# RWKV-7 recurrence in chunks of 64 tokens, directions in sequence, two tiles' inverses by common instructions

## Chip, cores, metric

The kernel runs on one core of a Trainium2 chip. The metric is the device time of the program in microseconds, the median of several runs. A profiled execution of the same program gives the trace.

## What is computed

One inference step of a layer: RMS norm and modulation, one input projection, a bidirectional RWKV-7 mixing group of 8 heads of 64 channels and a bidirectional S5 group beside it, an output projection and an MLP, over 1024 latent and 128 context tokens. The part that matters here is the RWKV-7 scan, for each head and direction:

```python
def step(S, inp):
    r_t, w_t, k_t, v_t, ma_t, b_t = inp          # ma = -kk, b = kk * a
    sa = jnp.einsum('dbhij,dbhj->dbhi', S, ma_t)
    S = S * w_t[..., None, :] + sa[..., None] * b_t[..., None, :] + v_t[..., None] * k_t[..., None, :]
    return S, jnp.einsum('dbhij,dbhj->dbhi', S, r_t)
s_last, ys = lax.scan(step, jnp.moveaxis(s0.astype(f32), 1, 0), xs)   # direction 1 on flipped tokens
y = ys[0] + flip(ys[1])
```

The context's tokens are scanned first from a zero state, and their last state is an output; the latent tokens start from a cached state. All of this stage is computed in float32.

## The kernel before

The program is a sequence of stages. Each stage is a block in which every engine runs its own queue in order, with semaphores between them; behind the block GpSimd clears the stage's semaphores, one instruction each (`clear`, L328). `stage_rwkv` (L1651) runs a loop of four passes over groups of 128 channels (two heads): `stage_prepare`, `stage_chunks`, `stage_finish`.

`stage_prepare` (L993) makes, for each direction, four operands of 128 channels by 1152 tokens, `R.x[d]`, laid out as 9 tiles of 128 tokens with 4 operands each (a, r, b, k, already scaled by the decays), the values `R.v`, and per tile the factors `R.pre`, `R.post` and `R.step` by which the state is carried on.

`stage_chunks` (L1181) works through the tiles of 128 tokens. Both directions go side by side: a step takes the next tile of each. A tile has two parts of work. The inverse: `turn` (L1295) transposes b and k and makes b·a for the two halves of 64 tokens; `score` (L1308) makes the 128x512 products of all tokens with all, for both heads; VectorE masks them (L1487); `start_inverse`, and five levels of `merge_q` (L1325) and `merge_x` (L1335), build the inverse of a unit triangular matrix of 64 tokens, for both heads and both halves, by blocks of 2, 4, ... 64. Each level goes TensorE (`merge_q`), ScalarE (L1469, eviction), TensorE (`merge_x`), VectorE (L1554, addition). The small products are 64x64, on diagonal quarters of the array (`blocks`, L1289). The recurrence: `right_side` (L1346), `solve_first` (L1358) for the first half, `carry` to the second, `solve_second`, `advance` (the state after the tile) and `output` (L1391). In a step the recurrence of the former tile is interleaved with the inverse of the next one, at fixed places between the levels. So there are ten steps: one with inverses alone, eight with both, one with the recurrence alone. Steps 3 to 8 are run by a loop of three rounds with two steps each, whose tiles are addressed by registers; GpSimd copies each tile's operands to a fixed place first (L1265 to L1274), and clears y at the head of the stage (L1255), to which both directions add their output (L1528). GpSimd also makes the masked blocks of all levels in one product (L1279).

`stage_finish` (L1564) normalises `y`, adds the bonus, multiplies by the gate and transposes.

In the trace a float32 multiplication is two MATMUL records.

Of the kernel before, what the change touches and what calls it, by code (L numbers as in the profile page):

```python
# [14 lines left out]
P = 128  # L15
# [977 lines left out]
def stage_prepare(nc, M, ins, ct):  # L993
# [10 lines left out]
    m, tot, step = A.take(NB), A.take(NB), A.take(NB)  # L1004
# [3 lines left out]
    tiles = lambda v: v.rearrange("p (b t) -> p b t", b=NB)  # L1008
    three = lambda v: v.rearrange("p (g c) -> p g c", g=TG)
    with ExitStack() as ctx:  # L1010
# [109 lines left out]
        def _(dve):  # L1120
# [19 lines left out]
            for d in range(2):  # L1140
                x = R.x[d]
# [17 lines left out]
                op(stt(out=x[:, :, 2, :], in0=tiles(kn), scalar=-1.0, in1=tiles(a), op0=ALU.mult, op1=ALU.mult))  # L1159
                op(ts(x[:, :, 3, :], tiles(a), par[:, 1:2], omka, ALU.mult, ALU.add))  # L1160
                op(tt(x[:, :, 3, :], x[:, :, 3, :], tiles(k), ALU.mult))
                for n, (src, v) in enumerate(((kn, e), (r, t))):
                    dve.wait_ge(ev("exp"), 3 * d + n + 1)
                    tt(x[:, :, n, :], tiles(src), tiles(v), ALU.mult).then_inc(ev("x"), 1)
                dve.wait_ge(ev("exp"), 3 * d + 3)
                for n in (2, 3):
                    tt(x[:, :, n, :], x[:, :, n, :], tiles(e), ALU.mult).then_inc(ev("x"), 1)

                dve.wait_ge(ev("edge"), 2 * d + 2)
                op(nc.vector.tensor_copy(step, R.post[d]))  # L1170
                if d == 0:
                    op(tt(step[:, 0:LB - 1], R.post[d][:, 0:LB - 1], R.pre[d][:, 1:LB], ALU.mult))
                else:
                    op(tt(step[:, 1:LB], R.post[d][:, 1:LB], R.pre[d][:, 0:LB - 1], ALU.mult))
                op(tt(R.step[d], step.unsqueeze(2).broadcast_to([P, NB, 2]),
                      M.head_ind.unsqueeze(1).broadcast_to([P, NB, 2]), ALU.mult))
# [4 lines left out]
def stage_chunks(nc, M, ins, outs, ct):  # L1181

# [3 lines left out]
    D2, H2 = range(2), range(2)  # L1193
    double = lambda *shape: [[A.take(*shape) for _ in D2] for _ in range(2)]
    st = double(4, P)
    vs = double(P)
    tm = double(3, P)
    xx = double(2, 2, 64)
    ar = double(2, 2, P)
    mt = [[[A.take(2, 2, P) for _ in range(2)] for _ in D2] for _ in range(2)]  # L1200
    lo = [A.take(2, NLEV - 1, 64) for _ in D2]
    qs = [A.take(2, 64) for _ in D2]
    rs = [A.take(2, 64) for _ in D2]
    u = [A.take(2, 64) for _ in D2]
    p = [A.take(2, 64) for _ in D2]
    pt = [A.take(2, 64) for _ in D2]
    enter = [A.take(2) for _ in D2]
    h0 = A.take(2, 64)
    fin = A.take(2, 64)
    half = [slice(0, 64), slice(64, P)]  # L1210
    flat = lambda v: v.rearrange("p h c -> p (h c)")

    SPREAD, BESIDE = ((1, 0), (1, 1), (0, 0), (0, 1)), (1, 2)
    INV = lambda d: ps[:, 2 + d]
    REC = lambda d: ps[:, 4 + d]
    PROD = lambda d, j: ps[:, 6 * d + j]
    with ExitStack() as ctx:
# [3 lines left out]
        def steps(eng, body, new=False, old=False):  # L1223


            def known(s):
                latent = lambda t: (t, LB - 1 - t) if t >= 0 else (LB, LB)
                body(lambda o: s + o, s % 2, latent(s - 1) if s <= LB else None, latent(s - 2) if s else None)
            for s in range(3):
                known(s)  # L1230
            with eng.Fori(1, LB // 2) as i:
                count = [eng.snap(i * 2 + o) for o in range(4)]
                for s in (1, 2):
                    tiles = [None, None]
                    for n, wanted in enumerate((new, old)):
# [4 lines left out]
        def first(eng):  # L1240

            eng.wait_ge(ev("y_clear"), 1)
# [1003 lines left out]
```

## Time and profile before

| | us |
|---|---|
| median of 3 runs | 3204.84 (3203.38 to 3208.48) |
| the profiled execution | 3206.6 |
| its span, first to last instruction | 3204.8 |
| TensorE busy | 2222.1 (69%), 19956 records |
| VectorE busy | 1513.0 (47%) |
| ScalarE busy | 690.0 (22%) |
| GpSimd busy | 652.4 (20%) |
| mean granted TensorE clock | 0.832 |

The busy times are of the whole span; a stage can be bound by another engine than the program. Engines are named PE (TensorE), PEld (its weight loads), DVE (VectorE), ACT (ScalarE), POOL (GpSimd), SP (SyncE). A "q" behind a name is the engine's sequencer. Times in a timeline are microseconds from the span's start. The granted clock 1.00 is 2.4 GHz, 0.50 is 1.2 GHz.

### The profile page before, as it was taken

The numbers are of one execution on the slowest core, as the hardware profiler recorded it, in microseconds if no ns is written. First come the engines' busy times: TensorE is split into PE (matmuls) and PEld (weight loads), VectorE is DVE, ScalarE is ACT, GpSimd is POOL, SyncE is SP. The second block draws the span as 40 slices with busy tenths as digits, with TensorE's granted clock in tenths as the row PEclk, the third lists the DMA queues.
The fourth block names the chain that finished last, engine by engine and source line by source line (L and its number), as shares of the span: only waits on it lengthen the run. The fifth ranks groups of instructions, "written<-read, shape, count | busy, mean of one in ns | idle before, by whom it ended". The sixth has DMA issues, their size and how long they took to land. (4 is left out here: it accounts for less than half of the span.)

```text
span 3204.8 us, 49900 instructions
## 1 busy us (share of the span) xinstructions
PE 2222.1 (69%) x19956; PEld 1392.6 (43%) x19956; DVE 1513.0 (47%) x2768; ACT 690.0 (22%) x1436; POOL 652.4 (20%) x585
## 2 busy tenths in 40 slices
PE   7406411332374994579665995499479999999998
PEld 1104211232242773357543773277335555555553
DVE  0360679776306553555526552655334333332335
ACT  0211100111212331233213321233123321211221
POOL 0200613300211221022111211122042211110134
PEclk9657556665686997789877996699689999999999
DMA  7410000000000000000000000000233111100112
GB/s 266 168 35 26 7 1 7 7 7 18 20 23 1 3 1 18 7 3 1 2 23 2 2 0 25 1 3 0 94 118 132 53 53 53 53 18 36 53 47 99
DMA packets 61998, 119.09 MB, mean 37 GB/s; under 512 B 4359, under 2 KB 24327, under 8 KB 61451
## 3 DMA queue, kind: packets, MB, share of 16 engines
q1 hardware_dynamic: 61852, 116.92, 10.7%
q8 instruction: 120, 1.97, 0.3%
q14 instruction: 26, 0.21, 0.0%
HBM read 104.53 MB, written 10.27 MB: 36 GB/s over the span
## 5 line engine op out<-in xcount | busy, mean ns | idle before, releaser
L82 PE MATMUL psum<-arena 128*128 128x384 bf16 (+2 forms) x2244 | 742.1, 337 | 293.9 <-POOL arena L375 79.4
L83 PE MATMUL psum<-arena 128*128 128x384 bf16 (+2 forms) x2244 | 743.2, 338 | 0.0
L84 PE MATMUL psum<-arena 128*128 128x384 bf16 (+2 forms) x2244 | 743.1, 338 | 0.0
L82 PEld LDWEIGHTS psum<-arena 128*128 128x128 bf16 (+1 forms) x2244 | 227.1, 101 | 472.0 <-issue 80.4
L1292 PE MATMUL psum<-arena 64*64 64x64 f32 x8640 | 359.1, 222 | 27.6 <-ACT arena L1469 8.5
L1292 PEld LDWEIGHTS psum<-arena 64*64 64x64 f32 x8640 | 303.7, 134 | 68.6 <-issue 46.3
L84 PEld LDWEIGHTS psum<-arena 128*128 128x128 bf16 (+1 forms) x2244 | 226.9, 101 | 174.7 <-issue 16.1
L83 PEld LDWEIGHTS psum<-arena 128*128 128x128 bf16 (+1 forms) x2244 | 225.2, 100 | 172.3 <-issue 13.1
L2026 DVE TENSOR_TENSOR arena<-arena 128x384 f32<-128x384 f32 x96 | 103.2, 1075 | 236.5 <-ACT arena L1893 236.5
L724 PE MATMUL psum<-arena 128*16 128x128 f32 (+1 forms) x128 | 29.7, 319 | 265.4 <-ACT arena L667 265.4
L1469 ACT ACTIVATE arena<-psum 128x128 f32<-128x128 f32 x360 | 95.7, 278 | 415.1 <-PE psum L1292 411.0
L1554 DVE TENSOR_TENSOR arena<-arena,psum 128x256 f32<-128x256 f32 (+1 forms) x360 | 139.6, 395 | 64.2 <-PE psum L1292 58.0
L2041 DVE TENSOR_TENSOR arena<-arena,psum 128x512 f32<-128x512 f32 x108 | 74.5, 690 | 195.9 <-PE psum L84 195.9
L1313 PE MATMUL psum<-arena 128*128 128x512 f32 x288 | 157.0, 654 | 5.3 <-ACT arena L1441 5.3
L1302 PE MATMUL psum<-arena 128*128 128x128 f32 x144 | 32.5, 310 | 161.3 <-ACT arena L1449 153.2
L724 PEld LDWEIGHTS psum<-arena 128*16 128x16 f32 (+1 forms) x128 | 18.9, 177 | 268.3 <-issue 266.9
L1279 POOL TENSOR_TENSOR arena<-arena 128x640 f32<-128x640 f32 x72 | 97.6, 1374 | 138.5 <-ACT arena L1453 138.5
L1947 POOL TENSOR_TENSOR arena<-arena 128x1024 bf16<-128x1024 f32 x32 | 63.8, 2027 | 260.7 <-ACT arena L1873 260.7
L1953 POOL TENSOR_TENSOR arena<-arena 128x4096 bf16<-128x4096 f32 x8 | 59.5, 7437 | 279.9 <-ACT arena L1885 279.9
L636 POOL TENSOR_TENSOR arena<-arena 128x960 f32 (+1 forms) x32 | 70.9, 2247 | 165.7 <-PE psum L697 165.6
L1272 POOL COPY arena<-arena 128x128 f32 (+1 forms) x72 | 23.2, 322 | 388.6 <-PE psum L1398 388.6
L1487 DVE TENSOR_TENSOR arena<-psum,arena 128x512 f32<-128x512 f32 x144 | 95.2, 680 | 9.4 <-PE psum L1313 9.4
(295 smaller groups left out, 3386.0 us busy)
## 6 DMA issues: line engine op xcount, KB each, us to landing
arena<-in_w_ff SPq DMA_DIRECT2D x16, 2048.0 KB, 8.7
arena<-in_w_ada SPq DMA_DIRECT2D x12, 2048.0 KB, 8.0
arena<-in_x SPq DMA_DIRECT2D x18, 512.0 KB, 3.7
arena<-in_pos SPq DMA_DIRECT2D x18, 512.0 KB, 4.7
arena<-in_w_in SPq DMA_DIRECT2D x12, 512.0 KB, 4.1
x<-arena SPq DMA_DIRECT2D x9, 512.0 KB, 3.1
arena<-x SPq DMA_DIRECT2D x9, 512.0 KB, 3.3
out_y<-arena SPq DMA_DIRECT2D x9, 512.0 KB, 2.6
```

Of the source, the lines that this page charges most:

```text
L82: nc.tensor.matmul(out, whi, xhi, start=first, stop=False)
L83: nc.tensor.matmul(out, wlo, xhi, start=False, stop=False)
L84: return nc.tensor.matmul(out, whi, xlo, start=False, stop=last)
L636: mult = lambda o, x, y: nc.gpsimd.tensor_tensor(o, x, y, ALU.mult)
L1279: nc.gpsimd.tensor_tensor(lo[d], tm[q][d][:, 2].rearrange("p (h c) -> p h c", h=2).unsqueeze(2) .broadcast_to([P, 2, NLEV - 1, 64]), M.lev ...
L1292: last = mm(out[half[b]], lhs[half[b]], rhs[half[b]], start=True, stop=True)
L1313: mm(PROD(d, j), st[q][d][:, 2 + j], ar[q][d].rearrange("p h m t -> p (h m t)"), start=True, stop=True)\
L1469: nc.scalar.activation(flat(qs[d]), INV(d)[:, 0:P], ACT.Copy).then_inc(ev("q_read", d, l), 1)
L1487: tt(mt[q][d][j].rearrange("p h m t -> p (h m) t"), PROD(d, j).rearrange("p (m t) -> p m t", m=4), M.score_mask[:, d], ALU.mult).then_inc( ...
L1554: tt(xd, xd, z[:, :, ms], ALU.add).then_inc(ev("x", d, l), 1)
L2026: nc.vector.tensor_tensor(f[N % 3], f[N % 3], f[N % 3], ALU.mult).then_inc(ev("square"), 1)
L2041: nc.vector.tensor_tensor(a, a, ps[:, 6 + h, :], ALU.add).then_inc(ev("acc"), 1)
```

## The change

The order becomes a sequence of 18 units, a unit being one tile in one direction: the nine of direction 0 (context first), then the nine of direction 1. Units are taken in pairs, nine pairs in each pass, and the code of all is written out, with constant addresses. Both units' inverses are made by the same evictions and additions. The recurrence goes in chunks of 64 tokens, two for each unit, 36 in a row, each of `enter`, `solve` and `leave`. A body `i` holds the inverses of pair `i` and the four chunks of pair `i - 1`.

- Preparation stores `R.x[d]` as 8 slots of 64 tokens per tile, so that a and r of one half, and b and k of one half, are neighbours; `R.step` has one factor per tile.
- `score` makes, for each head and half, 128x128 products within the half (64 rows of the array, 128 columns). Six buffers `mt` hold the masked scores.
- The levels: `merge_q` for both units, then VectorE's `copy_predicated` puts the masked part into `grow` (an identity elsewhere, from GpSimd at the head), `merge_x` for both units, then ScalarE copies the whole bank to `xx`. GpSimd's product of all levels' blocks goes; it makes the first blocks `xt0` in eight small operations a pair.
- `turn` transposes b and k by multiplication with the identity, for `leave` alone.
- ScalarE writes each chunk's output to `R.y[d]`; nothing is added there. `stage_finish` adds the two directions at its head.
- The loop, the copies to a fixed place, the clearing of y and the wide masks go. The stage uses 46 semaphores instead of 107.

The core of the diff; what is left out is the old bodies and the counterparts of these functions on the other engines:

```diff
-                x = R.x[d]
+                x = [R.x[d][:, :, at] for at in (slice(1, 3), slice(0, 4, 3), slice(5, 7), slice(4, 8, 3))]
...
-                op(tt(R.step[d], step.unsqueeze(2).broadcast_to([P, NB, 2]),
-                      M.head_ind.unsqueeze(1).broadcast_to([P, NB, 2]), ALU.mult))
...
+def unit(u):
+    d, s = u // NB, u % NB
+    return d, s, LB if s == 0 else (s - 1 if d == 0 else LB - s)
...
+            def merge_q(i, l):
+                pe.wait_ge(ev("x0_read") if l == 1 else ev("x", l - 1), i + 1)
+                for q in H2:
+                    for h in H2:
+                        for f in H2:
+                            r = upper(f)
+                            last = mm(qblock(r, q, h), mt[(2 * i + q) % 6][r, h, f, 1 - f], xx[r, q, h, 0], start=True, stop=True)
+                last.then_inc(ev("q", l), 1)
+            def merge_x(i, l):
+                pe.wait_ge(ev("q_read", l), i + 1)
+                for q in H2:
+                    for h in H2:
+                        for f in H2:
+                            r = upper(f)
+                            xt = xt0[r, q, h] if l == 1 else xx[r, q, h, 1]
+                            if l < NLEV - 1:
+                                mm(xblock(r, q, h, 0), xt, grow[r, l - 1, q, h], start=True, stop=True)
+                            last = mm(xblock(r, q, h, 1), grow[r, l - 1, q, h], xt, start=True, stop=True)
+                last.then_inc(ev("xq", l), 1)
...
+            def enter(g):
+                pe.wait_ge(ev("state"), g + 1)
+                need(pe, ev("y_read"), g)
+                for h in H2:
+                    last = mm(MIX[upper(f), h, mixcol(f)], slot(x, f, 0)[half[h]], state[g % 4][half[h]], start=True, stop=True)
+                last.then_inc(ev("enter"), 1)
+            def solve(g):
+                pe.wait_ge(ev("w"), g + 1)
+                pe.wait_ge(ev("x_last"), g // 4 + 1)
+                for h in H2:
+                    last = mm(MIX[r, 0, 128 + 64 * h:192 + 64 * h], xf[par][r, q, h], w[g % 2][r, h], start=True, stop=True)
+                last.then_inc(ev("u"), 1)
+            def leave(g):
+                pe.wait_ge(ev("u_read"), g + 1)
+                pe.wait_ge(ev("uv"), 2 * (g // 2) + 2)
+                pe.wait_ge(ev("tm"), g // 4 + 1)
+                for h in H2:
+                    last = mm(PUT[half[h]], tm[par][q][:, f, half[h]], uv[par][q][:, f, half[h]], start=True, stop=True)
+                last.then_inc(ev("put"), 1)
+                for h in H2:
+                    mm(MIX[half[f], h, mixcol(f)], slot(x, f, 1)[half[h]], state[g % 4][half[h]], start=True, stop=False)
+                    last = mm(MIX[half[f], h, mixcol(f)], mt[g // 2 % 6][:, h, f, f], uv[par][q][:, f, half[h]],
+                              start=False, stop=True)
+                last.then_inc(ev("y"), 1)
...
+            def body(i):
+                inv, old, front = i < PAIRS, i > 0, i + 1 < PAIRS
+                g = 4 * (i - 1)
...
```

With both parts present, TensorE's order in a body is: leave(g-1), begin, enter(g), local, merge_q 1, solve(g), merge_x 1, leave(g), merge_q 2, enter(g+1), merge_x 2, solve(g+1), turn, merge_q 3, leave(g+1), merge_x 3, enter(g+2), score, merge_q 4, solve(g+2), merge_x 4, leave(g+2), score, merge_q 5, enter(g+3), merge_x 5, solve(g+3). The eviction of merge_q on VectorE (where both units have one direction), the first blocks on GpSimd, and the head of `stage_finish`:

```diff
+            def merged(i, l):
+                reset(i, l)
+                dve.wait_ge(ev("q", l), i + 1)
+                nc.vector.copy_predicated(grow[:, l - 1].rearrange("p q h c -> p (q h) c"),
+                                          where[:, 1 - d0, l:l + 1].broadcast_to([P, 4, 64]),
+                                          Q[:, 0:4 * 64].rearrange("p (b c) -> p b c", b=4)).then_inc(ev("q_read", l), 1)
...
+            def first_block(u):
+                pool.wait_ge(ev("masked"), u + 1)
+                need(pool, ev("xq", 1), u // 2)
+                for f in H2:
+                    r = upper(f)
+                    masked.step(tt(xt0[r, q], mt[u % 6][r, :, f, 1 - f], M.level_mask[r, d, 0:1].broadcast_to([64, 2, 64]),
+                                   ALU.mult))
+                    masked.settle(pool)
+                for f in H2:
+                    r = upper(f)
+                    first.step(tt(xt0[r, q], xt0[r, q], M.ident64[r].unsqueeze(1).broadcast_to([64, 2, 64]), ALU.add))
+                    first.settle(pool)
...
+            op(tt(y, y, R.y[1], ALU.add))
```

`xt0` must be there for `begin`, which is the start of the next pair's inverses; its scores are made in the body before.

## Rows read from the trace of the kernel before

**Rows 1.** Windows: stretch: us, busy us and records of each engine, PEclk, DMA share, GB/s.
```profile
1028.00:1240.00 212.00, 189.73 (x2916) 143.33 (x2916) 116.58 (x280) 64.69 (x216) 47.40 (x93) 0.97 0.01 2
1031.00:1035.00 4.00, 2.53 (x12) 1.17 (x12) 1.82 (x3) 2.33 (x8) 2.38 (x5) 0.50 0.01 2
1040.00:1050.00 10.00, 8.92 (x215) 7.53 (x216) 3.99 (x10) 2.69 (x10) 0.00 (x0) 1.00 0.01 2
1073.46:1095.10 21.64, 20.71 (x326) 15.78 (x326) 12.50 (x30) 7.21 (x25) 5.08 (x10) 1.00 0.01 3
1570.00:1577.00 7.00, 5.38 (x48) 4.64 (x46) 3.08 (x12) 0.00 (x0) 0.00 (x0) 1.00 0.00 0
1915.00:1922.00 7.00, 6.90 (x38) 6.64 (x37) 2.22 (x8) 0.00 (x0) 0.00 (x0) 0.52 0.00 0
315.00:335.00 20.00, 19.28 (x63) 11.21 (x63) 0.00 (x0) 5.90 (x11) 0.00 (x0) 0.50 0.00 1
```
**Rows 2.** Timeline of TensorE: start, duration; heads of two successive full steps.
```profile
1094.92 0.41 PE L1302 MATMUL psum<-arena 128*128 128x128 f32 x2 [0.20 <-DVE arena L1554]
...
1116.39 0.30 PE L1302 MATMUL psum<-arena 128*128 128x128 f32 x1 [0.21 <-DVE arena L1554]
```
**Rows 3.** Timeline: first and last operation of the first and third pass.
```profile
1028.10 1.06 POOL L1255 MEMSET arena<- 128x1152 f32 x1 [76.85 <-POOLq L330]
...
1232.18 0.28 DVE L1528 TENSOR_TENSOR arena<-arena,psum 128x128 f32<-128x128 f32 x1
...
1714.70 1.06 POOL L1255 MEMSET arena<- 128x1152 f32 x1 [76.85 <-POOLq L330]
...
1923.27 0.28 DVE L1528 TENSOR_TENSOR arena<-arena,psum 128x128 f32<-128x128 f32 x1
```
**Rows 4.** Timeline of TensorE: heads of the last step, same passes.
```profile
1224.16 0.46 PE L1353 MATMUL psum<-arena 128*128 128x128 f32 x2 [0.24 <-DVE arena L1554]
...
1912.25 0.46 PE L1353 MATMUL psum<-arena 128*128 128x128 f32 x2 [0.24 <-DVE arena L1554]
```
**Rows 5.** Timeline: one level of both directions' merges in the first step.
```profile
1043.72 0.28 ACT L1469 ACTIVATE arena<-psum 128x128 f32<-128x128 f32 x1 [1.68 <-PE psum L1292]
...
1045.92 0.28 ACT L1469 ACTIVATE arena<-psum 128x128 f32<-128x128 f32 x1 [1.45 <-PE psum L1292]
```
**Rows 6.** Timeline in a full step: 16 records on 64x64 quarters, twice.
```profile
1114.58 0.68 PE L1292 MATMUL psum<-arena 64*64 64x64 f32 x16
...
1115.50 0.68 PE L1292 MATMUL psum<-arena 64*64 64x64 f32 x16 [0.24 <-ACT arena L1469]
```
**Rows 7.** Groups by line and form: count, busy us, mean ns, idle before.
```profile
L1554 DVE TENSOR_TENSOR arena<-arena,psum 128x256 f32<-128x256 f32 x72 | 30.0, 422 | 11.1 <-PE psum L1292 9.7
L1469 ACT ACTIVATE arena<-psum 128x128 f32<-128x128 f32 x90 | 23.9, 278 | 103.8 <-PE psum L1292 102.8
L1487 DVE TENSOR_TENSOR arena<-psum,arena 128x512 f32<-128x512 f32 x34 | 22.4, 679 | 0.3 <-PE psum L1313 0.3
L1279 POOL TENSOR_TENSOR arena<-arena 128x640 f32<-128x640 f32 x16 | 21.6, 1370 | 32.4 <-ACT arena L1453 32.4
L1453 ACT ACTIVATE arena<-psum 128x384 f32<-128x384 f32 x16 | 7.9, 492 | 5.0 <-PE psum L1304 5.0
L1554 DVE TENSOR_TENSOR arena<-arena,psum 128x128 f32<-128x128 f32 x18 | 4.8, 289 | 4.9 <-PE psum L1292 4.8
L1272 POOL COPY arena<-arena 128x128 f32 x12 | 3.8, 317 | 83.4 <-PE psum L1398 83.4
L1606 ACT ACTIVATE arena<-psum 128x512 f32<-128x512 f32 x2 | 1.2, 599 | 17.1 <-PE psum L84 17.1
```
**Rows 8.** Timeline of TensorE: changes of form, in the S5 stage and in a full step.
```profile
315.72 0.45 PE L401 MATMUL psum<-arena 128*128 128x128 f32 x1 [10.71 <-ACT arena L365]
...
316.10 0.28 PE L402 MATMUL psum<-arena 16*128 16x16 f32 x1
...
1112.24 1.15 PE L1292 MATMUL psum<-arena 64*64 64x64 f32 x32
...
1113.32 0.49 PE L1395 MATMUL psum<-arena 128*128 128x128 f32 x2
```
**Rows 9.** Timeline: VectorE's products from SBUF, before and beside GpSimd's.
```profile
1117.73 0.29 DVE L1535 TENSOR_TENSOR arena<-arena 128x128 f32<-128x128 f32 x1 [1.23 <-ACT arena L1453]
...
1118.06 1.29 DVE L1538 TENSOR_TENSOR arena<-arena 128x128 f32<-128x128 f32 x1
```
**Rows 10.** Timeline at the stages' borders; one full-width addition of the final stage.
```profile
1025.18 0.18 DVE L1175 TENSOR_TENSOR arena<-arena 128x18 f32<-128x18 f32 x1
...
1028.27 2.11 DVE L1478 MEMSET arena<- 128x512 f32 x4 [2.91 <-PEq L330]
...
1240.94 1.35 DVE L1628 TENSOR_REDUCE arena<-arena 128x18 f32<-128x1152 f32 x1 [8.48 <-PEq L330]
...
1251.87 1.35 DVE L1636 TENSOR_TENSOR arena<-arena 128x1152 f32<-128x1152 f32 x1
```

More of the change, by code:

```diff
@@ L1003, in stage_prepare @@
     r, k, kn, a, lw, c_, e, t = (A.take(T) for _ in range(8))
-    m, tot, step = A.take(NB), A.take(NB), A.take(NB)
+    m, tot = A.take(NB), A.take(NB)
     hb = A.take(4)
@@ L1221, in stage_chunks @@
         block = ctx.enter_context(nc.Block())
[L1223 to L1235, printed above, removed]
-                        tiles[n] = (eng.snap(i * 2 + (s - 1 - n)), eng.snap(LB - s + n - i * 2)) if wanted else (i, i)
-                    body(lambda o, s=s: count[s + o], s % 2, *tiles)
-            known(LB + 1)
-        def first(eng):
-            eng.wait_ge(ev("y_clear"), 1)
         @block.sync
@@ L1433, in _, with score @@
-            pe.wait_ge(ev("p_clear"), 2)
-            steps(pe, body)
+            def score(u):
+                d, s, tile = unit(u)
+                q, x = u % 2, R.x[d][:, tile]
+                need(pe, ev("masked"), u)
+                if q == 0:
+                    need(pe, ev("lkv"), u)
+                for f in H2:
+                    for h in H2:
+                        at = 2 * P * q + P * f
+                        last = mm(SCORE[:, h, at:at + P], kb(x, f)[half[h]], ar(x, f)[half[h]], start=True, stop=True)
+                last.then_inc(ev("score"), 1)
@@ L1470, in _, with begun, local @@
-            act.wait_ge(ev("ar_clear"), 4)
-            steps(act, body)
+            copy = lambda out, src: nc.scalar.activation(out, src, ACT.Copy)
+            def begun(i):
+                act.wait_ge(ev("x0"), i + 1)
+                copy(xx[:, :, :, 0], X.rearrange("p (q h n c) -> p q h n c", q=2, h=2, n=2)[:, :, :, 0]).then_inc(ev("x0_read"), 1)
+            def local(i):
+                act.wait_ge(ev("local"), i + 1)
+                for f in H2:
+                    r = upper(f)
+                    src = ps[r, f, :].rearrange("p (q c) -> p q c", q=2)[:, :, 0:P]
+                    copy(wv[i % 2][r], src).then_inc(ev("lkv"), 1)
@@ L1560, in stage_chunks @@
+            nc.vector.memset(state[0], 0.0).then_inc(ev("state"), 1)
+            mask(0)
+            mask(1)
+            dve.wait_ge(ev("grow"), 1)
+            for i in range(PAIRS + 1):
+                body(i)
+            advanced(4 * PAIRS - 1)
     clear(nc, ev)
```

600 lines of the change are left out of this document (309 added, 291 removed).

## The prediction

> **What bounds the kernel now.** The page's slices and the windows by stage come first. The four passes of the recurrence stage (one for each group of two heads) are a quarter of the program: TensorE is busy 189.7 of 212 us in a pass, at a granted clock of 0.97 [rows 1]. The timeline of TensorE then shows what a step costs: a full step, from one turn of the operands to the next, takes 21.47 us [rows 2], and TensorE is busy 20.71 of 21.64 us in one [rows 1]. So before the change these stages are bound by TensorE's queue; VectorE (12.5 us a step), ScalarE (7.2) and GpSimd (5.1) have room [rows 1]. A pass runs from GpSimd's first MEMSET to VectorE's last addition: 204.4 us in the first and 208.9 in the third [rows 3]; the second and the fourth, read in the same way, lie between, and the mean of the four is 206.3. There are 8 full steps, a first one before them (inverses alone) and a last one (recurrence alone), 8.3 us [rows 4].
>
> The third pass is longer because its last step took 11.3 us against 8.3 [rows 4]: TensorE's granted clock there was 0.52, the 1.2 GHz level, against 1.00, the 2.4 GHz level, in the same step of the second pass [rows 1]. So in one pass the clock held through 7 us in which the engine was busy for 5.38, and in the other it fell in the same work. In the full steps and in the first step's merges (8.92 of 10 us busy) the clock stayed at 1.00 [rows 1].
>
> **The sizes of a hop.** In the first step the merges stand alone, and one level for both directions is 2.20 us (ACT at 1043.72, then at 1045.92) [rows 5]. The parts add up to that: 8 records on 64x64 quarters, half of such 16, take 0.45 us to their end (16 take 0.68, two quarters side by side [rows 6], and 32 take 1.15 [rows 8]), 0.04 to ScalarE's start, 0.28 for its copy [rows 7], 0.15 back to TensorE, 0.64 for 16 that wait for nothing else, 0.04 to VectorE, 0.42 for the addition of 256 columns [rows 7], 0.15 back: 2.17. So I trust such sums for the new chain. Evictions by columns: ScalarE 0.28 for 128, 0.49 for 384, 0.60 for 512, hence 0.385 for 256; VectorE 0.29 for 128, 0.42 for 256, 0.68 for 512, hence 0.22 for 64 [rows 7].
>
> **What one change of form costs on TensorE.** Where a matrix multiplication has another number of active rows or columns than the one before, it starts 0.07 us before the former's end and never earlier: 316.10 against an end at 316.17, and 1113.32 against 1113.39 [rows 8]; without a change the next pair of records follows 0.058 after the start of the former (32 records in 1.15). I found this at every change of form at which work was waiting, some 600 of them, all with 128x128 or 16x128 on one side. The new recurrence alternates 64x64 with 128x64, which no row shows directly. The Trainium skill, "TensorEngine Tiling (Array Packing)", Key Properties, says that a change of tiling mode drains TensorE; by that rule every alternation pays, and the trace agrees for the forms that it shows.
>
> **The new body, for two tiles of one direction.** TensorE's records do not get fewer: 180 multiplications or 360 records a body, against 326 for two tiles before [rows 1]. What falls is the 128x512 scores and the count of evictions; what is added is a recurrence of 4 successive steps a body, in place of two directions side by side.
> One level of both inverses at once: merge_q 16 records, 0.67; 0.04; copy_predicated of 256 columns, 0.42; 0.15; merge_x 32 records, 1.14; 0.04; ScalarE's copy of 512 columns, 0.60; 0.15: 3.21 us. copy_predicated is in no row: I take the addition of 256 columns, as it reads as many PSUM columns; the ends are the 128-column addition, 0.29, and the 512-column product, 0.68.
> One `leave` is put, then state part and score part for each head in turn: 128x64, 64x64, 128x64, 64x64, 128x64. Each piece is two records (0.107 to the second) and then the change (0.218 less 0.07): 0.255, five times, 1.28 us. Four leaves are 5.1 us of TensorE a body.
> Beside a level's ScalarE or VectorE hop TensorE has 0.8 to 0.9 us free. In the order of the code: begin to the first merge 1.24; level 1 3.21 and 0.42 because leave(g) doesn't fit; level 2 3.21 and 0.40 for the turn (8 records at 0.112 and two changes); level 3 3.21 and 0.60 for leave(g+1); level 4 3.21 and 1.00 for leave(g+2) and a score; level 5 to the end of the next leave 4.10 (merge_q, the predicated copy behind a mask, merge_x of 16, ScalarE 0.385 and 0.28 one after the other, leave 1.28). Sum 20.6 us against 21.47. TensorE is occupied 17 to 18 of it, so the four leaves decide.
> A pass: 7.0 us to the first begin (h0's DMA, the grow copy, and eight GpSimd operations of 0.40 with 0.10 between, where 640 columns take 1.37 and a copy of 128 0.32 [rows 7]); first body 16.9 (1.24, four levels, 2.8); 8 bodies of 20.6 and 1.5 in all for the resets and the split copies where the direction changes, 166.3; last, recurrence alone: 4 steps of 1.8 (leave, until ScalarE has freed the MIX columns), 0.79 (enter to solve) and 0.91 (solve to put), 13.8 with its end. Sum 204.0 at the full clock, 2.3 less than the mean before.
>
> **Clock.** The first body starts at 1.2 GHz, as before (0.50 in that stretch [rows 1]), but has no 128x512 scores ahead, and its merges wait more: at that level throughout it would cost 7.3 us more, at the other nothing; I take 4. In the full bodies TensorE is occupied some 0.87 of the time, as in the last steps of before, of which two of four fell, at 3.0 us a fall [rows 4]. If none falls, 0; if all run at 1.2 GHz, 30.2 us a body, so 77 a pass. I take about one fall a pass, 3.5; and 1.5 for the last body. Together 9.0 a pass.
>
> **GpSimd beside VectorE.** A VectorE product from two SBUF operands took 1.29 us beside GpSimd's 128x640 product [rows 9], against 0.29 for the one just before it. The predicated copy has its mask in SBUF and its data in PSUM, like the additions with a PSUM operand, which keep 0.42. The Trainium skill, "SBUF — State Buffer", says that GpSimd and a VectorE operation with two SBUF inputs exclude each other on one pair of ports; by it this copy goes free, and the trace agrees for the additions. I add 1.0 a pass for what the copy may be above 0.42 or held up (ends -4, +9, from the two rows).
>
> **Outside the pass.** After a pass GpSimd clears the stage's semaphores: VectorE is idle 8.48 us behind it, and 2.91 after the preparation [rows 10]. I count 107 semaphores and 28, so 0.07 us each; the new stage has 46, hence 4.0: 4.4 less. The final stage gains one addition of 1152 columns at its head, 1.35 and 0.04 [rows 10]: 1.4 more. Preparation writes the same columns in runs of 64 and loses two operations of 0.18 [rows 10]: 0.4 less; nothing hides any of these three. The clearing of y goes, 1.06 [rows 3], but h0's DMA is then late. Half of the score masks' constants go from the first DMA: nothing. Unrolling: steps in straight-line code took 21.6, in the loop 21.5 to 21.8 over its jump: nothing, ±0.3 a body.
>
> **Sum.** A pass: -2.3 + 9.0 + 1.0 - 4.4 + 1.4 - 0.4 = +4.3 us, four times +17. The profiled execution is 3206.6 us (span 3204.8), so 3223.8; the median of the runs is 1.8 below it: 3222.
>
> **Rivals.**
> (1) 64x64 and 128x64 follow each other without the drain. Leave is then some 0.7 us, a body 18.5 and a pass 185, 18.9 less: 3222 - 76 = 3146, faster. For: no row with that pair. Against: every other pair drains. It decides where a leave is under 0.9 us. 0.10.
> (2) As forecast, but the clock stays up or recovers within the first body: 9.0 a pass less, 3186, faster. For: the first body of before. 0.15.
> (3) The clock falls in a third or more of the full bodies: +25 a pass or more, 3322 and up (3500 if in all). For: the rows 315.72 on, where two forms alternate and TensorE is busy 19.28 of 20 us at a clock of 0.50 [rows 1, 8]. 0.17.
> (4) The predicated copy takes 0.68 or is held by GpSimd: +9 a pass, 3258. 0.08.
> (5) "Common instructions" don't overlap in TensorE's quarters (enter's and score's two row halves one after the other): 0.7 us a body, +24, 3246; kept in the forecast's own range, 3190 to 3265. Forecast 0.50, of which 0.08 below 3198 and 0.12 within 0.2%, which is about what a measurement of this kernel can tell from no change.
> Faster 0.33, same 0.12, slower 0.55. The range, 3150 to 3330, leaves out the lower part of (1) and the upper of (3).
>
> **What would show it.** In the new profile: begin to begin 20.6 us; the five pieces of a leave at 0.255; copy_predicated at 0.42; gap behind the pass 4.0; clock row of the passes. If leave is 0.7, rival 1; if the clock of a pass is under 0.85, rival 3; if the gap between merge_q's end and merge_x is above 0.7, rival 4. A body that is long by waits that I haven't named (GpSimd's first_block late for begin, which I put 1.6 us ahead of its need) would make the working wrong even at the right time.

## The result, and the profile after

| | us |
|---|---|
| median after | 3212.85 (3208.91 to 3219.81, 8 runs) |
| median before, same chip | 3204.19 (3200.61 to 3208.48, 8 runs) |
| ratio after/before | 1.0027, 95% [1.0016, 1.0037] |
| the profiled execution after | 3210.29, span 3208.5 |
| forecast | 3222 (3223.8 in the profile) |

The change makes the kernel slower, by 8.7 us (0.3%) in the medians and by 3.7 us between the two profiled executions; the forecast had 18 and 17. The sign and most terms stand, but the sum is more than twice too large. The windows of the four passes, from GpSimd's first operation to ScalarE's last, come first (columns as in [rows 1]).

```profile
1028.34:1242.25 213.91, 182.96 (x3240) 153.97 (x3240) 51.29 (x153) 59.59 (x162) 49.79 (x129) 0.89 0.01 3
1377.00:1587.17 210.17, 178.94 (x3240) 150.11 (x3240) 51.17 (x153) 59.59 (x162) 49.78 (x129) 0.91 0.01 3
1722.05:1932.47 210.42, 179.11 (x3240) 150.24 (x3240) 51.17 (x153) 59.59 (x162) 49.80 (x129) 0.91 0.01 3
2066.78:2277.38 210.60, 179.19 (x3240) 150.31 (x3240) 51.17 (x153) 59.59 (x162) 49.80 (x129) 0.91 0.01 3
```

A pass takes 211.3 us in the mean (206.3 before, 214.0 forecast). TensorE has more records (3240 against 2916 [rows 1]) and less busy time; VectorE's busy time is under half of what it was. The granted clock of a pass is 0.89 to 0.91, where it was 0.97 in the first pass [rows 1]. Where that clock goes is seen in shorter windows of TensorE alone (its busy time, PEclk, DMA share, GB/s): the start of the first body of the second pass, the piece in which it comes back, a full body, the head of the second body of the first pass, and the last body.

```profile
1384.00:1394.00 10.00, 8.15 (x130) 0.50 0.01 2
1394.00:1399.00 5.00, 4.42 (x66) 0.70 0.00 0
1405.00:1425.39 20.39, 18.47 (x360) 1.00 0.01 2
1058.00:1062.00 4.00, 3.80 (x78) 0.63 0.01 4
1572.00:1587.00 15.00, 11.26 (x68) 0.50 0.00 1
```

The full bodies run at 2.4 GHz nearly throughout. In this pass the inverses' first 13 us are at 1.2 GHz: the mean of 0.70 between 1394 and 1399 puts the clock's return at 1397, and the first begin is at 1383.76. The last body is at 1.2 GHz in all four passes, but for its first 1 us. In the first pass the clock fell twice within full bodies (windows with all engines, columns as in [rows 1]):

```profile
1059.10:1062.40 3.30, 3.15 (x50) 2.97 (x51) 0.44 (x1) 1.02 (x3) 0.00 (x0) 0.50 0.02 5
1062.60:1079.50 16.90, 15.38 (x277) 12.78 (x272) 4.80 (x14) 4.83 (x13) 5.33 (x14) 1.00 0.01 2
1079.60:1082.90 3.30, 3.17 (x58) 2.99 (x60) 0.74 (x2) 1.61 (x5) 0.00 (x0) 0.50 0.00 0
```

Each fall lasted 3.4 us, and the two bodies took 21.57 and 21.33 in place of 20.39: 1.2 and 0.9 us more. The timeline of the second pass gives the lengths: GpSimd's first operation, the heads of the first four bodies and of the eighth full one (`begin`, L1259), ScalarE's last.

```profile
1377.00 1.25 POOL L1484 COPY arena<-arena 128x1280 f32<-128x1280 f32 x1 [76.48 <-POOLq L330]
...
1383.76 0.80 PE L1259 MATMUL psum<-arena 64*64 64x64 f32 x10 [3.50 <-POOL arena L1501]
...
1405.01 0.51 PE L1259 MATMUL psum<-arena 64*64 64x64 f32 x10 [1.01 <-POOL arena L1501]
...
1425.40 0.27 PE L1259 MATMUL psum<-arena 64*64 64x64 f32 x2
...
1445.79 0.32 PE L1259 MATMUL psum<-arena 64*64 64x64 f32 x3
...
1549.52 0.68 PE L1259 MATMUL psum<-arena 64*64 64x64 f32 x16
...
1586.89 0.27 ACT L1405 ACTIVATE arena<-psum 64x128 f32<-64x128 f32 x1 [2.19 <-PE psum L1338]
```

The first begin comes 6.8 us after the start (forecast 7.0), the first body takes 21.25 (22.72 in the first pass), a full body 20.39 (forecast 20.6; the two with the direction's change and its resets take 21.2, two behind them 20.48), and from the eighth full body's head to the end it is 37.64. The row at 1405.01 has one thing more in its brackets: the second begin waited 1.01 us for GpSimd, a wait that the forecast had named only as a sign of being wrong.

One leave, in the second full body (to hold against [rows 8]):

```profile
1428.91 0.34 PE L1334 MATMUL psum<-arena 128*64 128x64 f32 x4
1429.18 0.33 PE L1337 MATMUL psum<-arena 64*64 64x64 f32 x2
1429.43 0.33 PE L1338 MATMUL psum<-arena 128*64 128x64 f32 x2
1429.69 0.32 PE L1337 MATMUL psum<-arena 64*64 64x64 f32 x2
1429.95 0.33 PE L1338 MATMUL psum<-arena 128*64 128x64 f32 x2
1430.20 0.68 PE L1280 MATMUL psum<-arena 64*64 64x64 f32 x16
```

Each piece starts 0.25 to 0.27 us after the former, 1.29 in all: the forecast's 5 x 0.255. (The forecast took each piece as two records. The put has four, and takes 0.27 all the same.) The groups by form in the first pass, and the borders of the final stage behind the second:

```profile
L1572 DVE COPY_PREDICATED arena<-arena,psum 128x256 f32<-128x256 int32 x40 | 17.7, 442 | 53.8 <-PE psum L1280 53.7
L1577 DVE COPY_PREDICATED arena<-arena,psum 128x128 f32<-128x128 int32 x10 | 2.5, 296 | 4.9 <-PE psum L1280 4.9
...
1591.06 1.36 DVE L1714 TENSOR_TENSOR arena<-arena 128x1152 f32<-128x1152 f32 x1 [5.61 <-PEq L330]
...
1596.64 1.35 DVE L1719 TENSOR_REDUCE arena<-arena 128x18 f32<-128x1152 f32 x1 [1.23 <-ACT arena L1695]
```

The predicated copy takes 0.44 (forecast 0.42), never more. From the end of the pass (1586.89 + 0.27) to 1591.06 it is 3.90 us (3.88 to 4.10 in the four), where it was 8.23 to 8.48; forecast 4.0.

### The profile page after: what moved, and what is told of

It is laid out like the page before. It is cut to its first block and busy times, and to the rows that moved or that the text cites. A ratio compares the mean times of both kernels' runs of the same rounds, so it can differ in the third digit from the quotient of the medians.

```text
span 3208.5 us, 50188 instructions
## 1 busy us (share of the span) xinstructions
PE 2174.9 (68%) x21252; PEld 1417.5 (44%) x21252; DVE 1253.9 (39%) x2256; ACT 669.6 (21%) x1220; POOL 663.4 (21%) x729
## 5 line engine op out<-in xcount | busy, mean ns | idle before, releaser
L1405 ACT ACTIVATE arena<-psum 64x128 f32<-64x128 f32 (+3 forms) x648 | 238.4, 380 | 628.7 <-PE psum L1293 302.0
L1292 PE MATMUL psum<-arena 64*64 64x64 f32 x2304 | 162.8, 233 | 44.0 <-DVE arena L1572 37.8
L1293 PE MATMUL psum<-arena 64*64 64x64 f32 x2880 | 180.1, 224 | 17.9 <-DVE arena L1572 14.9
L1293 PEld LDWEIGHTS psum<-arena 64*64 64x64 f32 x2880 | 158.1, 140 | 22.8 <-DVE arena L1572 19.3
L1292 PEld LDWEIGHTS psum<-arena 64*64 64x64 f32 x2304 | 137.4, 138 | 62.2 <-DVE arena L1572 52.4
L1572 DVE COPY_PREDICATED arena<-arena,psum 128x256 f32<-128x256 int32 x160 | 70.6, 441 | 212.0 <-PE psum L1280 211.5
L1248 PE MATMUL psum<-arena 64*128 64x128 f32 x576 | 56.1, 317 | 142.4 <-PEq L330 139.2
L1496 POOL TENSOR_TENSOR arena<-arena 64x128 f32<-64x128 f32 x144 | 64.8, 450 | 329.2 <-issue 258.3
L1280 PE MATMUL psum<-arena 64*64 64x64 f32 x2880 | 129.0, 232 | 5.6 <-ACT arena L1405 5.0
L1280 PEld LDWEIGHTS psum<-arena 64*64 64x64 f32 x2880 | 103.6, 141 | 24.7 <-ACT arena L1405 12.3
```

What stands on the lines that cost most here:

```text
L1280: last = mm(qblock(r, q, h), mt[(2 * i + q) % 6][r, h, f, 1 - f], xx[r, q, h, 0], start=True, stop=True)
L1292: mm(xblock(r, q, h, 0), xt, grow[r, l - 1, q, h], start=True, stop=True)
L1293: last = mm(xblock(r, q, h, 1), grow[r, l - 1, q, h], xt, start=True, stop=True)
L1405: copy = lambda out, src: nc.scalar.activation(out, src, ACT.Copy)
L1496: masked.step(tt(xt0[r, q], mt[u % 6][r, :, f, 1 - f], M.level_mask[r, d, 0:1].broadcast_to([64, 2, 64]), ALU.mult))
L1572: nc.vector.copy_predicated(grow[:, l - 1].rearrange("p q h c -> p (q h) c"), where[:, 1 - d0, l:l + 1].broadcast_to([P, 4, 64]), Q[:, 0:4 ...
```

## Experiments

Times are medians, ratios are against the kernel before on the same chip. Unless said otherwise the base is the kernel after.

### The changes of form: two runs

```diff
                 for h in H2:
-                    mm(MIX[half[f], h, mixcol(f)], slot(x, f, 1)[half[h]], state[g % 4][half[h]], start=True, stop=False)
-                    last = mm(MIX[half[f], h, mixcol(f)], mt[g // 2 % 6][:, h, f, f], uv[par][q][:, f, half[h]],
-                              start=False, stop=True)
+                    mm(MIX[half[f], h, mixcol(f)], mt[g // 2 % 6][:, h, f, f], uv[par][q][:, f, half[h]],
+                       start=True, stop=False)
+                for h in H2:
+                    last = mm(MIX[half[f], h, mixcol(f)], slot(x, f, 1)[half[h]], state[g % 4][half[h]], start=False, stop=True)
```

The second run has the same two loops with the state parts first, as in the code of the change (four changes of form).

> The changed kernel, with the order inside a leave turned round: put, then the score parts of both heads, then the state parts of both heads, so that TensorE changes its form twice in a leave in place of six times; same multiplications, same waits. Theory A (each change of form drains TensorE and leaves sit on the path): a leave is 6 records at 0.058 apart and 4 such with two changes, 0.76 us against 1.28; four of them a body give 20.4 - 2.2 = 18.2 to 18.4 us from begin to begin, 19.5 us less a pass, about 3210 - 78 = 3132 us in the profile, 0.976 of the kernel before. Rival B (the changes of form lie beside the evictions' waits and cost the body nothing): body 20.4, 3210 us. In between, if the score now stands in the way of the next merges: body near 19.3, 3172 us.

> The changed kernel with a leave ordered as put, both state parts, both score parts: four changes of form in place of six. Theory A (cost goes by the number of changes): a body of 18.8 to 19.0 us, 14 us less a pass, about 3210 - 57 = 3153 us; two thirds to three quarters of what two changes give. Rival B (not the changes but the waits decide): the same time as the changed kernel, 3210. If a gain comes from the order of the parts alone and not from the number of changes, this one and the one with two changes give the same.

Measured: 3122.3 us (3118.3 to 3123.4), ratio 0.9741 [0.9724, 0.9758]; and 3161.8 us, 0.9868 [0.9852, 0.9885]. A full body takes 17.98 with two changes and 18.83 with four, against 20.39 with six: 2.4 and 1.56 less. A leave of the first, and the heads of two bodies:

```profile
1710.66 0.34 PE L1334 MATMUL psum<-arena 128*64 128x64 f32 x4
1710.83 0.40 PE L1337 MATMUL psum<-arena 128*64 128x64 f32 x4
1711.15 0.33 PE L1340 MATMUL psum<-arena 64*64 64x64 f32 x4
1711.42 0.68 PE L1280 MATMUL psum<-arena 64*64 64x64 f32 x16
...
1725.02 0.27 PE L1259 MATMUL psum<-arena 64*64 64x64 f32 x1
...
1743.00 0.27 PE L1259 MATMUL psum<-arena 64*64 64x64 f32 x1
```

And the same leave in the second run, with four changes:

```profile
1391.65 0.34 PE L1334 MATMUL psum<-arena 128*64 128x64 f32 x4
1391.91 0.33 PE L1337 MATMUL psum<-arena 64*64 64x64 f32 x4
1392.18 0.45 PE L1339 MATMUL psum<-arena 128*64 128x64 f32 x4
1392.55 0.68 PE L1280 MATMUL psum<-arena 64*64 64x64 f32 x16
```

The same six multiplications take 1.29 us with six changes, 0.90 with four and 0.76 with two. The four leaves of a full body, each from its put to the next work, take 5.17, 3.60 and 2.69 together: 1.57 and 2.48 less, which is what the bodies lose, 1.56 and 2.41. Theory A holds for both in this: the drain between 64x64 and 128x64 is real (the forecast's first rival is out), and the leaves lie on the path. The price does not go by the number of changes alone, though. A put is followed after 0.27 us by another form and after 0.17 by its own, so one change costs 0.10. The larger part of what the second run gains is that like parts are neighbours: the state parts of both heads, four records, take 0.27 together, where two records took 0.26. A score part adds to what the state part wrote, which would be another cause of its late start; but the next state part, which adds to nothing, starts as late (0.26 and 0.26 in the rows of the change), so that is not it. The rule of the Trainium skill, "TensorEngine Tiling (Array Packing)", Key Properties, that a change of tiling mode drains the engine, holds here too, between two modes that both use 64 columns; the page gives no price, these rows give 0.10 us for one change alone and 0.53 for the whole leave.

### What the common instructions are worth

```diff
-                    copy(xx.rearrange("p q h n c -> p (q h n c)"), X).then_inc(ev("x", l), 1)
+                    for q in H2:
+                        last = copy(xx[:, q].rearrange("p h n c -> p (h n c)"), X[:, 2 * P * q:2 * P * q + 2 * P])
+                    last.then_inc(ev("x", l), 1)
...
-                if d0 == d1:
+                if False:
```

> The changed kernel, in which ScalarE and VectorE evict the inverses of the two directions' tiles by an instruction for each tile (two of 256 columns in place of one of 512; two predicated copies of 128 in place of one of 256), TensorE's work unchanged. Theory A (the level's chain of evictions sets the body, so common instructions are what gained): ScalarE 2 x 0.38 + 0.05 against 0.597 and VectorE 2 x 0.298 against 0.441 give 0.3 to 0.37 a level; the levels that have no TensorE work to hide it give 0.9 us a body, 7.7 a pass, 3210 + 31 = 3241 us. Rival B (TensorE's own queue sets the body and covers the evictions): 3210 us within 4.

(The first and the last copy of a body are split in the same way.)

Measured: 3231.4 us (3230.4 to 3232.3), 1.0084 [1.0067, 1.0101], 18.5 above the change: half of A's 31. A full body is 20.80, so 0.4 longer and not 0.9. The pairs of instructions show why (ScalarE, then VectorE):

```profile
1454.05 0.66 ACT L1405 ACTIVATE arena<-psum 128x256 f32<-128x256 f32 x2 [1.37 <-PE psum L1293]
...
1452.00 0.50 DVE L1583 COPY_PREDICATED arena<-arena,psum 128x128 f32<-128x128 int32 x2 [1.18 <-PE psum L1280]
```

Two copies of 256 columns take 0.66 together, where one takes 0.38 and one of 512 takes 0.60; two predicated copies of 128 take 0.50, where one takes 0.30 and one of 256 takes 0.44. So an instruction starts before the former's end, and the split costs 0.06 + 0.06 a level, not 0.35. The Trainium skill has figures for both engines: "ScalarE: Activation LUTs", What ACT_TABLE_LOAD costs, has successive ACTIVATEs overlap by about 93 ns; in these rows it is 0.10 us (twice 0.38 less 0.66). "Vector Engine (DVE) Microarchitecture Reference", 5.2, gives VectorE 1.0417 ns a column and about 75 ns an instruction in a queue, so by it a second copy of 128 columns would add 0.21 us, an estimate; in these rows it adds 0.20. Eight bodies a pass make 13 us of the 18.5. For the other 5.5 the trace has falls of the clock: one body took 25.91 us, with a fall of 13.7 us in it, and five others 0.9 more than their like, 9.5 us in all against 2.1 in the trace of the change.

### The clearing of semaphores

```diff
+            for n in range(61):
+                ev("idle", n)
```

> The changed kernel with 61 more semaphores in the recurrence stage's list, which nobody signals and which are cleared with the others behind each pass, 107 in all as in the kernel before. Theory A (the gap behind a pass is GpSimd clearing one semaphore after another, 0.07 us each): gap 8.2 to 8.5 in place of 3.9 to 4.1, 4.4 us a pass, 3210 + 17.5 = 3227.5 us, 1.0055 of the changed kernel. Rival B (the gap of before was the loop's end or the transfers, not the count): gap unchanged, 3210 us.

Measured: 3229.0 us (3225.8 to 3232.8), 1.0079 [1.0061, 1.0098], 16.2 more than the change. The same border as above:

```profile
1599.24 1.36 DVE L1716 TENSOR_TENSOR arena<-arena 128x1152 f32<-128x1152 f32 x1 [9.43 <-PEq L330]
```

The pass ended at 1591.53, so the gap is 7.71 in place of 3.90: 0.062 us for each of 61. Theory A stands, the price a little under the 0.07 taken; the run below with 15 fewer has 2.82, 0.072 for each. But with the 107 semaphores of before the gap is 7.7 us and not 8.2 to 8.5: the count makes 3.8 us of the 4.35 by which the gap shrank, and the other 0.5 stays unexplained.

### The addition in the final stage

```diff
-            op(tt(y, y, R.y[1], ALU.add))
```

> The changed kernel without the addition of the two directions' outputs at the head of the final stage (1152 columns on VectorE; the output of the second direction is left out of the result). Theory A (nothing hides it, as forecast): 1.39 us a pass less, 3210 - 5.6 = 3204.7 us. Rival B (TensorE's gate work and ScalarE's copies in that stage end later than the addition, so part of it was hidden; the stage grew by 0.9 and not 1.4 between the two kernels): 0.9 a pass or less, 3206.5 to 3210 us.

Measured: 3211.7 us (3205.6 to 3221.4, 12 runs), 1.0019 [1.0010, 1.0028]: too near to the change to tell in the total, the more so as the profiled execution (3216.6) had seven short falls of the clock and that of the change two. The rows of the stage tell: from the end of the second pass to GpSimd's first operation of the final stage, a power that waits for VectorE's sums, it is 10.14 us in place of 11.12, 0.98 less. VectorE's second sum of this run:

```profile
1594.85 1.35 DVE L1718 TENSOR_REDUCE arena<-arena 128x18 f32<-128x1152 f32 x1 [1.65 <-ACT arena L1695]
```

It waits 1.65 us for ScalarE's square, against 1.23 with the addition: without the addition ScalarE is still evicting the gates when the square's input is ready, and 0.4 of the addition's 1.39 lay beside that. Rival B, nearly: 0.98 where it had 0.9 or less.

### The clock at the head and at the tail of a pass: two runs

```diff
+            def fill(tiles, bank):
+                for b in H2:
+                    mm(ps[half[b], bank, 0:tiles * P], M.ident64[half[b]], R.v[half[b], 0:tiles].rearrange("p b c -> p (b c)"),
+                       start=True, stop=True)
...
                     merge_x(i, 1)
+                    if i == 0:
+                        fill(2, 5)
```

(the same behind levels 2 to 4, and `fill(4, 5)` twice before the first body; in the second run `fill(2, 4)` behind each `enter` and `solve` of the last body alone)

> The changed kernel, with multiplications that nobody reads put into TensorE's idle time before the first begin (4 of 64x512 in all) and behind each of the first four levels of a pass's first body (2 of 64x256 each), so that the engine waits less there. In the changed kernel the first body ran at a granted clock of 0.50 for its first 10 to 13 us and took 21.24 us (22.7 in the first pass). Theory A (the engine's waits in that body keep the clock down, and a filled one gets it back earlier): first body 17 to 19 us, 2 to 4 us less a pass, 3210 - 8 to 17 = 3193 to 3202 us. Rival B (the clock comes back when it does, whatever the engine did): the fillers cost what they take at the low clock where they stand in a merge's way, 0 to 2 us a pass more, 3210 to 3218 us.

> The changed kernel, with multiplications that nobody reads (2 of 64x256) behind each enter and each solve of a pass's last body, where TensorE waits for VectorE and ScalarE. In the changed kernel that body ran at a granted clock of 0.50 in all four passes and took 37.67 us from its begin of the eighth full body to the end, 3.3 more than worked out at the full clock. Theory A (the waits of the last body make the clock fall): begin of the eighth to the end 34.4 to 35.5, 2 to 3.3 us less a pass, 3210 - 9 to 13 = 3197 to 3201 us. Rival B (it falls for what came before, in the eighth full body, or the fillers don't suffice): the fillers stand in the way of solve and leave at the low clock, 0 to 3 us a pass more, 3210 to 3222 us.

Head: 3197.3 us (3194.7 to 3200.4, 10 runs), 0.9975 [0.9966, 0.9984], so 0.25% faster than the kernel before. The first body takes 18.12 in all four passes:

```profile
1377.90 0.27 PE L1259 MATMUL psum<-arena 64*64 64x64 f32 x2 [0.55 <-POOL arena L1517]
...
1396.01 0.51 PE L1259 MATMUL psum<-arena 64*64 64x64 f32 x10 [1.13 <-POOL arena L1517]
```

Theory A: the granted clock is 1.00 from the first begin on, where it was 0.50 for 13 us. The second begin still waits 1.13 us for GpSimd, so that is no matter of the clock.

Tail: 3213.1 us (3198.5 to 3218.1), 1.0024 [1.0008, 1.0040], no different from the change. Behind it stand two cases. From the eighth head to the end the passes took 39.91, 39.75, 33.56 and 33.55 us, against 37.76 in the mean without fillers; the second and the third (windows in the last body, columns as in [rows 1]):

```profile
1571.00:1586.00 15.00, 13.64 (x86) 8.38 (x84) 1.60 (x6) 1.64 (x6) 0.59 (x2) 0.50 0.00 1
1918.00:1933.00 15.00, 12.63 (x132) 7.63 (x128) 2.28 (x9) 2.84 (x10) 0.59 (x2) 1.00 0.01 1
```

In two passes the clock stayed at 1.00 and 4.2 us were gained, in two it fell all the same and the fillers cost 2.1. Neither theory alone; what tells the two cases apart stays open. (The two in which it stayed up are those whose first body took the long 22.6 to 22.7; no run shows whether the one hangs on the other.)

### Do more waits bring the clock of the full bodies down?

```diff
+    spare = A.take(4 * P)
...
+                    copy(spare, X)
                     copy(xx.rearrange("p q h n c -> p (q h n c)"), X).then_inc(ev("x", l), 1)
```

> The changed kernel in which ScalarE evicts the inverses' X twice in levels 1 to 4 (once to a tile nobody reads), 0.45 to 0.6 us more in each, so that TensorE waits longer in every full body. Theory A (waits of that size don't bring the clock down; the body only grows by them): 21.6 to 22.8 us a full body, +10 to 19 us a pass, 3250 to 3287 us. Rival B (the third rival of the forecast: with more waits the clock falls in a third or more of the full bodies): 25 us and more for those, 3330 us and up.

Measured: 3231.8 us (3230.7 to 3233.6), 1.0081 [1.0062, 1.0099], under what either theory gave. A pair of copies takes 1.08 in place of 0.60:

```profile
1453.08 1.08 ACT L1406 ACTIVATE arena<-psum 128x512 f32<-128x512 f32 x2 [1.34 <-PE psum L1294]
```

Four times 0.49 are put in, and a full body grows by 0.49; by the order of the code, TensorE's leaves, turn and scores stand beside the copies of the other levels. Of the 28 full bodies that can be read from head to head, eight took a further 0.9, each with one fall of 3.4 us in it. So there are two falls a pass with more waits, in this one trace, and one costs about 1 us, not the 10 of a body that is all at 1.2 GHz: the engine is back at 2.4 GHz within the body. That is where rival 3 of the forecast fails, by its price.

### The late first blocks, and a better kernel: four runs

Fifteen semaphores fewer (one count for all levels in place of one each), with the grouped leaves:

```diff
-                pe.wait_ge(ev("q_read", l), i + 1)
+                pe.wait_ge(ev("q_read"), 5 * i + l)
```

and for the others, in the first body only, the same with `mask` on VectorE:

```diff
                     merge_x(i, 1)
+                if i == 0:
+                    score(2)
...
                     merge_x(i, 2)
+                if i == 0:
+                    score(3)
...
-                if front:
+                if front and old:
                     score(2 * i + 2)
```

> The kernel with the parts of a leave grouped (two changes of form in place of six, 3122.3 us median, 3123 in its profile) and, beside it, 15 semaphores fewer in the recurrence stage: those of the five levels are one count each (31 in all in place of 46). Theory A (clearing costs 0.07 us each): the gap behind a pass 2.9 in place of 4.0 us, 4.3 us less in all, 3118 us; 0.9728 of the kernel before. Rival B (15 fewer change nothing, or the counts cost in the body): 3122 us or above.

> The changed kernel with the early scores and masks of tiles 2 and 3 in the first body alone, no fillers, leaves and semaphores as in the change. Theory A (GpSimd's masking of the first blocks is what the second begin waits for, 1.0 us in the trace, at either clock): 1 us less a pass, 3210 - 4 = 3206 us; the wait of the second begin for GpSimd gone. And if the busier start brings the clock back earlier, up to 3 us more a pass, 3194 us. Rival B (another wait comes last there): first body unchanged at 21.2 us, 3210 us.

> The kernel with grouped leaves and 15 semaphores fewer (3113 us median), with two more edits in each pass's first body only: the scores and masks of tiles 2 and 3 come behind levels 1 and 2 in place of 3 and 4, and fillers (multiplications nobody reads) stand before the first begin and behind levels 3 and 4. Theory A: with the clock up, the first body is 18.1 us because the second begin waits 1.1 us for GpSimd, which masks the first blocks of tiles 2 and 3 only after their late scores; with early scores that wait goes and the body is 16.9 to 17.3 us against 21.2 to 22.7, 4 us less a pass: 3113 - 16 = 3097 us, 0.967 of the kernel before. Rival B (the early scores and masks stand in the way of merges, or the clock doesn't come back): 18 to 21 us for the body, 3100 to 3113 us.

> The kernel of the run called early, and the fillers behind each enter and solve of the last body as well. In the changed kernel those fillers kept the clock up in two passes of four (33.6 us from the eighth begin to the end against 37.7) and cost 2.2 us in the two in which it fell. Theory A (with bodies less full of waits ahead of it the clock holds): 3 to 4 us less a pass, 3097 - 14 = 3083 us. Rival B (as often up as down): 1 us less a pass, 3093 us. Rival C (it falls always, for what comes before): 2.2 more a pass, 3106 us.

| run | median | ratio, 95% |
|---|---|---|
| grouped_few | 3112.9 (3108.6 to 3130.0) | 0.9727 [0.9702, 0.9751] |
| early_only | 3205.9 (3200.8 to 3211.3) | 1.0002 [0.9991, 1.0013] |
| early | 3097.5 (3095.0 to 3098.1) | 0.9660 [0.9645, 0.9674] |
| early_tail | 3088.2 (3086.5 to 3095.6, 5 runs) | 0.9630 [0.9615, 0.9645] |

(One further execution of the last took 8093 us; why is not known. With it the median is 3089.2.)

Fewer semaphores: theory A (the gap is above). One execution of four took 3130.0, the others 3108.6 to 3113.5.

```profile
1667.67 0.27 PE L1259 MATMUL psum<-arena 64*64 64x64 f32 x2
...
1684.80 0.27 PE L1259 MATMUL psum<-arena 64*64 64x64 f32 x2 [0.57 <-ACT arena L1422]
```

These are the first two heads of a pass of the run early: the wait for GpSimd is gone, ScalarE's eviction of the last level comes last now, and the first body takes 17.13 in all four passes, against 18.12 with late scores and 21.25 without fillers. Theory A, for the body (16.9 to 17.3) and the time (3097). Without fillers (early_only) the wait for GpSimd is gone too, and three first bodies of four took 19.2 to 19.4: with the scores as work in that place the clock was back 7 us behind the first begin and not 13. The time is what A gave without help of the clock (3206): of the 2 us that these three bodies gained by the clock, a fall of 1 us in the full bodies of each pass took back half. With fillers in the tail as well, the stretch from the eighth head to the end took 29.26, 31.73, 34.93 and 29.26 us, against 32.5 to 32.6: 1.3 us a pass less in the mean. That trace is of the slowest of the five executions; in the medians the gain is 9.3 us, between theories A (14) and B (4), and the two ratios' intervals just touch. Splitting the two tiles' chains so that one merges while the other is evicted wasn't tried.

## Why the prediction was right in sign and wrong in size

A pass, in us, by the forecast's terms:

| term | forecast | measured | from |
|---|---|---|---|
| start to first begin | 7.0 | 6.9 | profile after |
| first body, full clock | 16.9 | 18.1 | fill_head |
| its clock | 4.0 | 3.5 | 21.25 three times, 22.72 once, less 18.12 |
| eight full bodies | 166.3 | 165.0 | heads of the second pass, 144.5 for seven, 20.5 |
| falls of the clock in them | 3.5 | 0.5 | two falls, 2.1 us, in one pass of four |
| last body, full clock | 13.8 | 13.1 | fill_tail, 33.56 less 20.48 |
| its clock | 1.5 | 4.2 | mean 37.76 less 33.56 |
| predicated copy | 1.0 | 0 | groups by form |
| sum | 214.0 | 211.3 | |
| gap behind the pass | -4.4 | -4.35 | |
| final stage and preparation | +1.0 | +0.45 | mean of three: +0.88, +0.67, -0.19 |

So a pass with what lies around it costs 1.1 us more than before, and not 4.3; four of them 4.4, where the spans differ by 3.7.

**What held.** The length of a leave and its place on the path; the level's sum (begin to begin 20.39 against 20.6); the gap by the count of semaphores, but for 0.5 us; the predicated copy. The structure costs about what it saves: a full body is 20.39 against 21.47 [rows 2] for the same two tiles, and the recurrence alone and the two ends take it back.

**The step that failed** is the price of a fall in the term "Clock" for the full bodies: "I take about one fall a pass, 3.5". The price came from the last steps of before, where the third pass took 3.0 us more [rows 4] (the fourth, the other that fell, 2.1). But there nothing but that step was left, and the clock stayed down to its end; in a full body it is back after 3.4 us. In 16 passes with these full bodies (four traces: after, idle_sems, fill_tail, no_add) it fell 15 times, each time for 3.4 us: once in three passes, twice, some 20 us apart, in six, not at all in seven. A pass with one fall is 1.0 us longer, one with two 2.1 to 2.2. So there are 0.94 falls a pass, about the one that I took, but a fall costs 1.0 us and not 3.5, which makes 1.0 us a pass in the mean. In the profiled execution this term alone is 3.0 of the 3.2 us by which the sum for a pass is too large. Longer falls exist, in two traces of altered kernels (10.2 us, which cost 3.7, in grouped; 13.7 us, which cost 5.1, in two_evictions). The likeness was wrong as well: I set the full bodies, busy for 18.5 of 20.39 us, beside the last steps of before, where the engine was busy for 5.38 of 7 us at the full clock [rows 1].

In these 16 passes falls and first bodies go together: each of the seven passes whose first body took the long 22.6 to 22.8 us had one or two behind it, of the nine with the short first body only two had. That is no rule, as fill_head has two passes with two falls behind first bodies of 18.1 us; what decides isn't shown. The profiled execution had only two falls in its four passes (0.5 us a pass), and of its first bodies one in four was long, against 7 in 16: it lies below the median of its runs, which is part of why the medians differ by 8.7 us and the two profiles by 3.7.

**The other misses** nearly cancel: the last body's clock, +2.7 (it falls in every pass; TensorE, with the recurrence alone, is busy for 11.3 of 15 us there); the first body, +1.2, of which 1.0 is GpSimd's first_block. I had put that 1.6 us ahead of its need; in the full bodies no begin waits for it, but in the first one there is no recurrence, the levels follow faster, and scores at levels 3 and 4 are too late. Against them stand the bodies at the full clock, -2.0 (the full ones -1.3, the last -0.7), and the margin for the copy, -1.0: the row of [rows 9] with its 1.29 us had both operands in SBUF, and no copy from PSUM was held up. The first body's clock is -0.5. A third of the final stage's addition was hidden by ScalarE, which I had denied.

## To carry to other kernels

Count the changes of form on TensorE along the path before counting its records: grouping the six multiplications of a leave by form took 2.4 us from each of eight full bodies a pass and 3.2 from the last, at 1.2 GHz, 90 us in all, more than the whole change moved. Like forms next to each other gain twice: no change between them, and their parts run side by side. Price a fall of the clock by what follows it: at the end of a pass it lasted to the end, in the midst of steady work it was over after 3.4 us in most cases and cost 1 us. And where the engine must wait at the start of a stage, real work moved up (scores, here) or fillers bring the clock back; what is last behind it then has to be looked up anew.

## What was not expected of the hardware

- On ScalarE and VectorE an instruction that waits for nothing starts about 0.1 us before the former's end: 0.66 us for two copies of 256 columns, 1.08 for two of 512, 0.50 for two predicated copies of 128. Splitting an eviction in two cost 0.06 us, not the 0.16 by which two durations exceed one.
- The first body's length has two values when nothing fills it, 21.1 to 21.3 and 22.6 to 22.8 us, for the same work; and with fillers the stretch from the eighth head to the end came out at 33.56 or 39.8. The granted clock of TensorE differs between them; what decides it wasn't found.
- A predicated copy from PSUM costs about what an addition of the same columns costs (0.44 for 256 against 0.42, 0.30 for 128 against 0.29 [rows 7]).
